# Retention's normalisation moved into the attentions, gated attention's turning moved behind the first branch's products

## What is computed

```python
u = rms_norm(x, mix_norm[l])
y_a = swa_sink_mixer(a_q, a_k, a_v, ...)           # banded attention with sinks
y_b = short_conv_mixer(b_x, b_b, b_c, conv_w[l])
y_c = nsa_mixer(c_q, ..., c_g, ...)                # compressed, selected and window attention, gated and summed
y_d = retention_mixer(d_q, d_k, d_v, d_g, ret_norm_gain[l])
branch = einsum('btnw,nwd->btnd', stack([y_a, y_b, y_c, y_d]), w_branch[l])
gates = sigmoid(gate_logits + merge_gate_bias[l])
x = x + sum(gates * branch, axis=2) @ w_out[l]
```

```python
mu = mean(o, axis=-1); var = mean(square(o - mu), axis=-1)
y_d = silu(gate) * (merge_heads((o - mu) * rsqrt(var + EPS)) * norm_gain)
```

## Time and profile before

| | us |
|---|---|
| median of 3 runs | 2968.07 |
| lowest, highest | 2967.51, 2973.12 |
| the profiled execution, its time | 2980.04 |
| the profiled execution, its span | 2978.3 |
| TensorE busy | 2795.8 (94%) |
| VectorE busy | 523.7 |
| ScalarE busy | 358.7 |
| GpSimd busy | 71.0 |

### The profile page before, as it was taken

One profiled execution on the slowest core, in us unless ns is written; L12 is line 12 of the kernel. 1 busy time (PEld: TensorE's weight loads), 2 busy tenths in 40 slices (PEclk: granted clock), 3 DMA queues, 4 the chain that ended last, 5 costly groups with the idle time before them and its releaser, 6 DMA issues. The chain is left out here.

```text
span 2978.3 us, 34705 instructions
## 1 busy us (share of the span) xinstructions
PE 2795.8 (94%) x15057; PEld 2179.7 (73%) x15057; DVE 523.7 (18%) x1134; ACT 358.7 (12%) x796; POOL 71.0 (2%) x87
## 2 busy tenths in 40 slices
PE   7999889989988998999998899999999998899999
PEld 5675455545544555888886788888888886788888
DVE  1421000010010001111223411111111224411111
ACT  2320010110011001000112301000000112301000
POOL 0000000000000000000200000000000200000000
PEclk9987777777787678999998999999999998999999
DMA  9547999999999999345552144445345552144340
GB/s 361 195 170 320 426 428 429 430 428 428 428 428 428 415 429 391 113 142 163 162 165 92 57 142 160 138 155 166 131 148 163 158 178 77 58 168 142 128 155 29
DMA packets 250666, 694.23 MB, mean 233 GB/s; under 512 B 12897, under 2 KB 194513, under 8 KB 225873
## 3 DMA queue, kind: packets, MB, share of 16 engines
q1 hardware_dynamic: 248112, 688.54, 61.1%
q10 hardware_dynamic: 2464, 4.39, 0.4%
HBM read 691.85 MB, written 1.05 MB: 233 GB/s over the span
## 5 line engine op out<-in xcount | busy, mean ns | idle before, releaser
L1068 PE MATMUL banks<-ZT,ring 128*128 128x256 f32 x2816 | 625.2, 380 | 1.3 <-ACT ZT L1524 1.3
L1068 PEld LDWEIGHTS banks<-ZT,ring 128*128 128x128 f32 x2816 | 535.7, 191 | 75.7 <-issue 1.8
L1084 PE MATMUL banks<-ZP,ring 128*128 128x256 f32 x1408 | 316.9, 379 | 0.0
L979 PE MATMUL banks<-ring,BK 128*32 128x512 f32 x2048 | 239.3, 613 | 61.4 <-DMA ring<-in_w 37.1
L1084 PEld LDWEIGHTS banks<-ZP,ring 128*128 128x128 f32 x1408 | 267.5, 190 | 36.4
L1281 PE MATMUL banks<-ZT,ring 128*128 128x256 f32 x1024 | 238.3, 387 | 0.0
L979 PEld LDWEIGHTS banks<-ring,BK 128*32 128x32 f32 x2048 | 66.4, 111 | 221.5 <-issue 126.3
L1281 PEld LDWEIGHTS banks<-ZT,ring 128*128 128x128 f32 x1024 | 197.3, 195 | 27.9 <-issue 0.4
L2012 DVE TENSOR_TENSOR ZP<-banks,RB 128x512 f32<-128x512 f32 x88 | 60.9, 692 | 686.7 <-PE banks L1068 686.5
L1004 PE MATMUL banks<-ring,GB 128*32 128x512 f32 x1024 | 179.9, 852 | 0.0
L1567 ACT ACTIVATE ZP<-ZP 128x256 f32<-128x256 f32 x88 | 36.6, 416 | 839.2 <-DVE ZP L2012 839.2
(11 more groups left out here) (339 smaller groups left out, 2214.2 us busy)
## 6 DMA issues: line engine op xcount, KB each, us to landing
ring<-in_w SPq DMA_DIRECT2D x192, 2048.0 KB, 18.0
ring<-in_w_in SPq DMA_DIRECT2D x79, 1024.0 KB, 5.0
ring<-in_ffn_w_gate SPq DMA_DIRECT2D x44, 1024.0 KB, 5.2
ring<-in_ffn_w_up SPq DMA_DIRECT2D x44, 1024.0 KB, 7.6
ring<-in_ffn_w_down SPq DMA_DIRECT2D x44, 1024.0 KB, 4.8
ring<-in_w_mod SPq DMA_DIRECT2D x24, 1024.0 KB, 11.6
ring<-in_w_branch SPq DMA_DIRECT2D x16, 1024.0 KB, 6.2
ring<-in_w_out SPq DMA_DIRECT2D x12, 1024.0 KB, 5.0
```

The costliest lines, as they stand in the source:

```text
L979: last = mm(ps[32 * j:32 * j + 32, 4 + b, :], XE[:, k, :], slot(n)[:, 512 * b:512 * b + 512], start=(k < 4), stop=(k >= 4))
L1068: last = mm(ps[:, 4 + q % 4, 256 * w:256 * w + 256], slot(n + w)[:, 256 * k + P * (q % 2):256 * k + P * (q % 2) + P], ZT[:, k, :], start=( ...
L1084: last = mm(ps[:, c // 2, 256 * (c % 2):256 * (c % 2) + 256], slot(n + 2)[:, D * (q % 2) + P * c:D * (q % 2) + P * c + P], FH[:, q % 4, :] ...
```

## The change

Four squares with sums by head (`head_variance`, 128 columns each, `accum_out` into the new `rss`) follow ScalarE's copy of the probabilities of units 0 and 1 of the first attention; VectorE's sum (L2277) goes, and GpSimd's `root` waits for the eight squares. VectorE scales the retention (`head_scales`) after unit 1 of the second attention. TensorE turns it (`turn_yd`, now in banks 4 and 5) behind the scores of unit 0 of the third attention, and waits for `yd_out` behind the gate's sums of that unit, ahead of the turning of its probabilities. VectorE multiplies with gain and gate (`retention_out`) between the maximum of unit 1 and the copy of unit 0 there. After the third attention the branches start at once. The wait for the last stored gate stands ahead of q = 2. y_c is turned ahead of q = 8; ScalarE copies it ahead of the sigmoid of q = 12; TensorE waits for these copies ahead of q = 24.

```diff
--- before.py
+++ after.py
@@ -230,6 +230,7 @@
         rcol = small[:, 428:430]
         rfin = small[:, 430:432]
         rtmp = small[:, 432:434]
+        rss = small[:, 448:456]
 
 
         landed = [sem(f"unit_landed{i}") for i in range(RING)]
@@ -355,7 +356,6 @@
         ret_rstd = sem("ret_rstd")
         ret_scores = sem("ret_scores")
         ret_squares = sem("ret_squares")
-        ret_sums = sem("ret_sums")
         rope_ready = sem("rope_ready")
         scattered = sem("scattered")
         sel_ready = sem("sel_ready")
@@ -804,7 +804,7 @@
                 last.then_inc(turn_full, 1)
 
 
-            def attention(units, base, scores, between, first=None):
+            def attention(units, base, scores, between, first=None, lead=None):
                 def turn(i, unit):
                     heads, keys = unit[1], unit[2]
                     pe.wait_ge(exp_done, base + (i + 1))
@@ -838,6 +838,8 @@
                     scores(i, unit)
 
                 score(0, units[0])
+                if lead:
+                    lead()
                 for i, unit in enumerate(units):
                     if i + 1 < len(units):
                         score(i + 1, units[i + 1])
@@ -885,14 +887,14 @@
                               start=True, stop=True)
                 last.then_inc(gm_full, 1)
 
-            def turn_y(tiles, src, done, base):
+            def turn_y(tiles, src, done, base, bank=2):
 
                 for n, j in enumerate(tiles):
                     if n >= 2:
                         pe.wait_ge(done, base + (n - 1))
                     for c in range(2):
                         for t in range(TT):
-                            last = tr(ps[:, 2 + n % 2, 256 * c + P * t:256 * c + P * t + P],
+                            last = tr(ps[:, bank + n % 2, 256 * c + P * t:256 * c + P * t + P],
                                       src[:, t, j + P * c:j + P * c + P], ident)
                     last.then_inc(y_full, 1)
 
@@ -1288,9 +1290,19 @@
                     pe.wait_ge(att_scaled, l * 12 + (8 + q - 1)) if q >= 2 else pe.wait_ge(att_scaled, l * 12 + 8)
                     gate_sums(q, ps[:, 6 + q % 2, 256:512])
 
-                def causal(qT, kind, col, base, early):
+                def turn_yd():
+
+                    pe.wait_ge(ret_normed, l + 1)
+                    turn_y((PB_DQ, PB_DQ + 256), PB, yd_out, l * 2, 4)
+
+                def causal(qT, kind, col, base, early, lead=None):
+                    def between(i):
+                        early_gate(early + i)
+                        if lead and i == 0:
+                            pe.wait_ge(yd_out, l * 2 + 2)
+
                     attention([(t, 4, t + 1, value2(col, g), g) for t in range(TT) for g in range(2)], base,
-                              scores2(qT, kind), lambda i: early_gate(early + i))
+                              scores2(qT, kind), between, lead=lead)
 
                 ya = l * 4 + 4
                 causal(aqT, 0, PB_AV, ua, 0)
@@ -1320,21 +1332,20 @@
 
                 pe.wait_ge(y_out, ya + 2)
                 causal(cqT, 1, PB_VS, ua + 4, 4)
-                causal(cqT, 2, PB_VW, ua + 8, 8)
-                pe.wait_ge(att_scaled, ua + 12)
-                pe.wait_ge(y_out, ya + 2)
-                turn_y((PB_CQ, PB_CQ + 256), PB, y_out, ya + 2)
-                pe.wait_ge(y_out, ya + 4)
-                pe.wait_ge(ret_normed, l + 1)
-                turn_y((PB_DQ, PB_DQ + 256), PB, yd_out, l * 2)
-
-
-                pe.wait_ge(yd_out, l * 2 + 2)
+                causal(cqT, 2, PB_VW, ua + 8, 8, turn_yd)
+
+
                 pe.wait_ge(conv_ready, l * 4 + 4)
-                pe.wait_ge(gate_stored, l * EARLY + EARLY)
                 for i, b in enumerate(BRANCHES):
+                    if i == 1:
+                        pe.wait_ge(att_scaled, ua + 12)
+                        turn_y((PB_CQ, PB_CQ + 256), PB, y_out, ya + 2)
+                    if i == 3:
+                        pe.wait_ge(y_out, ya + 4)
                     for c in range(KC):
                         q = 8 * i + c
+                        if q == 2:
+                            pe.wait_ge(gate_stored, l * EARLY + EARLY)
                         br = U_LAYER + L_GATE + branch_unit(i)
                         if q >= 4:
                             pe.wait_ge(merged, l * 32 + (q - 3))
@@ -1479,7 +1490,7 @@
             turn_copy(QT[:, 0:512], 3, 2)
             turn_copy(QT[:, 1024:1536], 5, 0)
 
-            def attention(units, base, first, exps):
+            def attention(units, base, first, exps, between=None):
                 def pt_copy(i):
                     n = units[i][1] * units[i][2] // 2 * P
                     act.wait_ge(p_turned, base * 2 + (2 * i + 1))
@@ -1499,6 +1510,8 @@
                     pt_copy(i)
                     if first:
                         part_copy(4 + i)
+                    if between:
+                        between(i)
 
             def exps1(i, unit):
                 b = i % 2
@@ -1643,7 +1656,18 @@
                     return exps
 
                 units = [(t, 4, t + 1) for t in range(TT) for g in range(2)]
-                attention(units, ua, False, exps2(True))
+                def head_variance(i):
+
+                    if i == 0:
+                        act.wait_ge(ret_centred, l + 1)
+                    if i == 1:
+                        act.wait_ge(ret_squares, l * 8 + 4)
+                    if i < 2:
+                        for h in range(4):
+                            fn(GBf[:, P * h:P * h + P], PB[:, i, PB_DQ + P * h:PB_DQ + P * h + P], ACT.Square, scale=P ** -0.5,
+                               accum_out=rss[:, 4 * i + h:4 * i + h + 1]).then_inc(ret_squares, 1)
+
+                attention(units, ua, False, exps2(True), head_variance)
                 for n in range(2):
                     y_copy(YT[:, 0, 2 * n:2 * n + 2, :], n, l * 6 + (4 + n + 1))
                 act.wait_ge(cmp_shifted, l + 1)
@@ -1653,17 +1677,13 @@
                 attention(units, ua + 4, False, exps2(False))
                 attention(units, ua + 8, False, exps2(False))
 
-                act.wait_ge(att_full, ua + 12)
-                act.wait_ge(ret_centred, l + 1)
-                fn(PR[:, 0, :].rearrange("p (t n) -> p t n", t=TT), PB[:, :, PB_DQ:PB_DQ + 512], ACT.Square,
-                   scale=P ** -0.5).then_inc(ret_squares, 1)
-                for n in range(2):
-                    y_copy(YT[:, 2, 2 * n:2 * n + 2, :], n, l * 6 + (6 + n + 1))
-
 
                 for i, b in enumerate(BRANCHES):
                     for c in range(KC):
                         q = 8 * i + c
+                        if q == EARLY:
+                            for n in range(2):
+                                y_copy(YT[:, 2, 2 * n:2 * n + 2, :], n, l * 6 + (8 + n + 1))
                         if q < EARLY:
                             act.wait_ge(gate_stored, l * EARLY + (q + 1))
                             fn(EG[q], EG[q], ACT.Sigmoid, bias=vc("merge")(KC * b + c)).then_inc(gate_ready, 1)
@@ -1821,7 +1841,7 @@
                 stt(out=v, in0=v, scalar=hrs[:, 28 + t:29 + t], in1=vgain, op0=ALU.mult, op1=ALU.mult
                     ).then_inc(vv_ready, 1)
 
-            def attention(units, base, first, maxima, scale_out):
+            def attention(units, base, first, maxima, scale_out, lead=None, between=None):
                 def row_maximum(i):
                     dve.wait_ge(scores_full, base + (i + 1))
                     if i >= 2 or not first:
@@ -2268,22 +2292,27 @@
                        over3(cden.rearrange("p (r t h) -> p t r h", t=TT, r=2)[:, t], HD), ALU.mult).then_inc(cmp_out, 1)
                 dve.wait_ge(cmp_out, l * 2 + 2)
 
-                attention(units, ua + 4, False, maxima2(("causal0", "causal1"), False), scale2(ua + 4, PB_CQ, 1, 4))
+                def head_scales(i):
+
+                    if i == 1:
+                        dve.wait_ge(ret_rstd, l + 1)
+                        tt(ro, ro, over3(hrs[:, 0:8].rearrange("p (t h) -> p t h", t=TT), P), ALU.mult).then_inc(ret_normed, 1)
+
+                def retention_out():
+
+                    for n in range(2):
+                        dve.wait_ge(y_full, l * 6 + (6 + n + 1))
+                        for c in range(2):
+                            y = YT[:, 3, 2 * n + c, :]
+                            last = stt(out=y, in0=ps[:, 4 + n, 256 * c:256 * c + 256], scalar=vc("ret", 2 * n + c), in1=y,
+                                       op0=ALU.mult, op1=ALU.mult)
+                            last.then_inc(yd_out, 1) if c else own(last)
+
+                attention(units, ua + 4, False, maxima2(("causal0", "causal1"), False), scale2(ua + 4, PB_CQ, 1, 4),
+                          between=head_scales)
                 dve.wait_ge(att_scaled, ua + 8)
-                attention(units, ua + 8, False, maxima2(("causal0", "causal1"), False), scale2(ua + 8, PB_CQ, 2, 8))
-
-
-                dve.wait_ge(ret_squares, l + 1)
```

(16 more changed lines are left out.)

## The result

| | kernel before | changed kernel |
|---|---|---|
| median, 20 runs of each | 2979.19 us | 2961.85 us |
| lowest to highest | 2967.51 to 2986.58 | 2956.12 to 2968.48 |
| ratio, 95% interval | | 0.995 (0.9938 to 0.9962) |
| the profiled execution's span | 2978.3 | 2955.4 |

The change makes the kernel faster by 0.5%: 17.3 us by the medians, 15 us by the ratio, whose interval reaches from 11 to 18.5 us. I had forecast -17.2 us and 2950.9 us. The size of the difference is near the forecast, in part by luck: a cost that I had held unlikely (rival 1) came, and a part of it was given back in places that no edit touched. The time lies 2.9 us above my range, because the kernel before is a kernel of 2979 us and not of the 2968.07 that three runs had shown.

A forecast was written before the change was run, and what follows sets the result against it. TensorE, busy 94% of the span, was taken to bound the kernel. Per layer -8.67 - 2.98 + 1.09 + 1.22 + 0.76 = -8.58 us, -17.2 for two, off the median 2968.07: 2950.9 us; range 2945 to 2959.

The forecast's parts named there:

- rival 1: Second attention: clock falls at TensorE's wait, grown to 1.91 us; costs 3.4 us a layer, 2957.7 us in all; chance 0.16.
- The base: Whole kernel: forecast taken off the unprofiled median of 2968.07 us, giving 2950.9; off the profiled 2980.04 us, 2962.8.
- The gap: Between the third attention's last weighing and the first branch product: the stretch of 8.67 us goes, -8.67 us a layer.
- The clock at the branches: At the 13 branch products: full clock returns, 22.49 us in place of 25.47, -2.98 us a layer.
- (a): In the branches: gated attention's output turned ahead of q = 8, 8 transposes on TensorE, +1.09 us a layer.
- (b): First attention: eight squares on ScalarE, hidden in its idle time without a table load, cost nothing; uncovered, 4.0 us a layer.
- (c): Second attention: VectorE's scaling between unit 1's output and unit 3's row maximum lengthens TensorE's wait, +1.22 us a layer.
- (d): Third attention: the retention's turning and four multiplications make the first weighing later, +0.76 us a layer.
- My own sign for it: Second and third attention: the prediction is wrong if the granted clock falls between 2540 and 2580 us.
- The sum: All terms together: -8.58 us a layer, -17.2 us for two layers; the forecast's chance was 0.72.
- Rivals 2 to 5: Clock fall lasting 13.7 us (0.04); weights late (0.03); wait holds first branch products (0.03); clock stays low, 3013 us (0.02).

The follow-up runs named there:

- after_again: The changed kernel, not altered, run and profiled once more; 2960.3 us, ratio 0.9945 to the kernel before.
- filled_gap: Kernel before plus unread transposes (8, 24 and 6 a layer) where TensorE waits behind the third attention; 2978.9 us, ratio 0.9995; repeated, 2979.5 us, 0.9999.
- scale_u2: Changed kernel with VectorE's scaling of the retention behind unit 2 instead of unit 1 of the second attention; 2956.8 us, ratio 0.9935 to the kernel before.
- scale_twice: Changed kernel with the retention scaled twice behind unit 1 of the second attention, first into an unread place; 2966.6 us, ratio 0.9966 to the kernel before.
- late_turn: Changed kernel with scaling behind unit 2 of the second attention, retention turned and multiplied in unit 2 of the third; 2955.7 us, ratio 0.9932 to before.
- norm_only: Changed kernel with both turnings and the multiplication back behind the third attention, only the normalisation moved; 2971.8 us, ratio 0.9976 to the kernel before.
- cq_first: Changed kernel with gated attention's output turned ahead of the branches again; 2964.7 us, ratio 0.9955 to the kernel before.

## Why the prediction was right in the change and wrong in the time

**The base** is the step that failed, where I wrote "off the median, 2950.9". I read the 12 us between the profiled 2980.04 and the median 2968.07 as something that a profile adds, and moved the sum over to the median of three runs. The runs show that the three were at the fast end of a kernel that spreads from 2964 to 2989 us around 2979, and that a profiled execution is one like the others (2961.52 against a median of 2960.3 in after_again). By the profiled execution's own time the sum had given 2962.8; measured are 2961.85. That this is so near is luck in part, since the sum had no fall of the clock in it. The range was built from the costs of the edits alone, 2945 to 2959, and had nothing in it for the base, though the rows showed two values 12 us apart for one kernel.

**The gap**, forecast -8.67: the first product starts 0.17 ahead of the last weighing's listed end (2566.14 + 1.90 to 2567.87), so -8.8. Nothing that I had read as done in time was late; the gate store and the merge were covered.

**The clock at the branches**, forecast -2.98: 13 products and the turning between them take 23.4 us (2567.87 to 2591.25), 22.5 of it the products'. filled_gap shows the cause by itself: -2.9 with the gap in place.

**(a)** Forecast +1.09: the turning adds 0.9 to 1.0. **(b)** Forecast nothing: the squares take 1.2 us a group, with no table load, so Square needs none beside Exp here. The one load there is that of the sigmoids. The price of 2.66 us for a switch of sets, which the prediction takes from the Trainium skill, "ScalarE: Activation LUTs", section "What ACT_TABLE_LOAD costs", doesn't show in it either: the load takes 1.28 us, and the sigmoid starts 1.29 us after the load's start (2563.07 to 2564.36). **(c)** Forecast +1.22: the wait grows from 0.69 to 1.80, +1.11, all of it on TensorE; scale_u2 and scale_twice show the same 1.1 taken away and doubled. **(d)** Forecast +0.76: 7.04 instead of 6.24, +0.80; late_turn takes it away. The way there is not quite the forecast one. VectorE's multiplications take 1.65 and not 1.73 and end at 2544.08, while TensorE is still in the gate's sums, which the transposes follow at 2544.38; so TensorE doesn't wait for them, and the turning on TensorE alone makes the transposes later. (In the prediction 2555.20 + 1.73 is 2556.93 and not 2556.97, which changes nothing that counts.)

**Rival 1**, to which I had given 0.16 at a price of 3.4 us a layer, came, and is the second thing that the prediction had wrong. The third weighing to the next scores takes 7.99 us without it (scale_u2, and before: 2543.19 to 2551.18) and 11.32 and 9.64 with it, so it costs 3.3 us in layer 0 and 1.7 in layer 1; a low stretch stood there in both layers of the changed kernel's two profiles, of scale_twice and of norm_only, and in layer 0 of cq_first, but not in its layer 1; and in none of the sixteen layers with a wait of 0.69 there: before (profiled twice), scale_u2, late_turn and the four profiles with added transposes. I had held the work around the wait against it. My own sign for it, a granted clock that falls between 2540 and 2580, came true, since these times of the kernel before are the later half of the second attention and the third. The Trainium skill's page, "TensorE: Matmul & The Clock Gate", section "HAM oscillation — how this bites in real kernels", names long waits for data; here a wait of 1.8 us (2.9 in scale_twice) between full units of work went with a fall in nine of ten layers.

**The sum** with what was measured, in layer 0: -8.8 - 3.0 + 1.0 + 1.1 + 0.8 + 3.3 = -5.6, and in layer 1, with 1.7, -7.2. The stages became 6.9 and 8.9 us shorter. The remaining 1.3 and 1.7 us lie ahead of the lengthened wait, where the low stretches of the first attention and the compressed part stand otherwise in this execution: in layer 0 they last as long as before, 6.8 and 13.7 us, but the second starts 2.8 us earlier in the stage; in layer 1 the first lasts 3.4 us in place of 6.8. No edit stands behind them that I could name, and in after_again they lie differently again. So 3.0 us of what rival 1 took, 5.0, came back by chance. Both stages together give -15.8 us; the ratio gives -15. Rivals 2 to 5 did not come: no DMA wait from the branches to the end, no low stretch above 6.8 us from the second attention on.

## What to carry to other kernels

Before a forecast is set on a base, look at how far runs of the unchanged kernel lie apart; where a profiled execution and the median of a few runs disagree by more than the forecast, the base belongs into the range. When a step is moved off a wait of the bottleneck engine into work of another engine, look for the unit in which that engine waits itself: one unit later the same 1.2 us of VectorE were free, and on the late chain they cost nearly their length, and in most layers a fall of the clock with it. And judge an added instruction by the whole time too, since a stage can become shorter while another part, untouched, becomes longer.

## What the runs showed of the hardware

A wait of 1.8 us of TensorE with busy stretches on both sides went with a fall of the granted clock from 1.00 to 0.50, for 3.4 or 6.8 us, in seven of eight layers, and one of 2.9 us in two of two; the same place with 0.69 had none in sixteen layers. Transposes that nothing reads, 8, 24 and 6 of them, kept the clock at 1.00 through a gap of 8 us in all four layers profiled, and 24 of them in both; the same 38 behind the gap left the fall where it was. They also showed a price: with 38 added transposes a layer in the gap, late in TensorE's list, the experts' part, which ends 500 us ahead of the first of them, took 7 to 10 us more in both profiles, and the kernel as a whole was no faster than before in 23 runs, though its stages were 5.1 to 6.7 us shorter in each layer. I can't say why.
